# Differential attention in a hybrid encoder: both score maps of a query block in one place, past keys stored in front of new keys

## The reference, cut to what matters

```python
s1 = jnp.einsum('bqhd,bkhd->bhqk', q1, k1).astype(jnp.float32) * scale + bias
s2 = jnp.einsum('bqhd,bkhd->bhqk', q2, k2).astype(jnp.float32) * scale + bias
p = jax.nn.softmax(s1, axis=-1) - lam * jax.nn.softmax(s2, axis=-1)
return jnp.einsum('bhqk,bkhd->bqhd', p.astype(v.dtype), v)
```

## Time and profile before

| | |
|---|---|
| median of three runs | 1973.59 us |
| the profiled execution, its own time | 1973.13 us |
| span in the profile, first to last instruction | 1971.0 us |
| TensorE busy | 1923.3 us, 98% of the span |
| VectorE, ScalarE, GpSimd busy | 65%, 54%, 10% |
| granted TensorE clock, mean | 0.996 |

### The profile page before, as it was taken

The page is one execution under the profiler, slowest core; times in us unless marked ns, Lnnn a source line. Parts: engine busy times, 40 slices in busy tenths (PEclk is TensorE's granted clock), DMA queues, the critical chain, the costliest instruction groups (busy, mean ns, idle before and its releaser), DMA issues.

```text
span 1971.0 us, 37511 instructions
## 1 busy us (share of the span) xinstructions
PE 1923.3 (98%) x15310; PEld 1884.5 (96%) x15310; DVE 1277.1 (65%) x2334; ACT 1061.0 (54%) x1715; POOL 191.2 (10%) x242
## 2 busy tenths in 40 slices
PE   7999999999999999999999999999999999999997
PEld 6999999999998999999989999999999989999997
DVE  6657676765437866666667676767654388666666
ACT  5466666665236644444565757575732475444444
POOL 4312121100110000000041212120001000000000
PEclk9999999999999999999999999999999999999998
DMA  5323232322232332233313232323222323333231
GB/s 139 102 65 111 65 102 71 85 65 86 86 100 72 91 103 87 86 97 94 99 55 100 66 101 73 103 71 85 74 87 86 95 69 95 89 115 87 86 95 60
DMA packets 275710, 172.34 MB, mean 87 GB/s; under 512 B 7592, under 2 KB 271104, under 8 KB 275552
## 3 DMA queue, kind: packets, MB, share of 16 engines
q1 hardware_dynamic: 268000, 155.47, 27.0%
q0 software_dynamic: 7520, 14.59, 2.7%
q10 hardware_dynamic: 32, 0.04, 0.0%
HBM read 158.86 MB, written 11.21 MB: 86 GB/s over the span
## 4 chain that ended last, share of the span: by engine, by line
PE 80%; ACT 9%; DVE 7%; issue 3%; DMA 1%; SPq 0%; ACTq 0%; DVEq 0%
PE PJ L774 34%; PE PJ L1054 19%; PE PX L1115 13%; PE PJ L786 3%; PE PJ L956 3%; PE PX L989 2%; ACT w_hi L1287 2%; DVE w_lo L1842 1%; DVE T L1952 1%; PE PX L1007 1%; PE PX L1027 1%; PE PX L786 1%; DVE uc L2090 1%; DMA w_raw<-in_w_in 1%; ACT L1513 1%
## 5 line engine op out<-in xcount | busy, mean ns | idle before, releaser
L1842 DVE TENSOR_TENSOR w_lo<-w_raw,w_hi 128x1024 fp32r<-128x1024 f32 x236 | 299.2, 1270 | 188.9 <-ACT w_hi L1287 187.9
L1287 ACT ACTIVATE w_hi<-w_raw 128x1024 fp32r<-128x1024 f32 x236 | 247.4, 1052 | 209.9 <-DMA w_raw<-in_w_down 124.5
L774 PE MATMUL PJ<-h_hi,w_hi 128*128 128x272 f32 x1536 | 329.4, 296 | 2.5 <-DVE T L1952 1.9
L774 PE MATMUL PJ<-h_hi,w_lo 128*128 128x272 f32 x1536 | 316.6, 288 | 0.0
L774 PE MATMUL PJ<-h_lo,w_hi 128*128 128x272 f32 x1536 | 315.9, 287 | 0.0
L774 PEld LDWEIGHTS PJ<-h_hi,w_hi 128*128 128x128 f32 x1536 | 239.8, 188 | 10.2 <-issue 7.4
L774 PEld LDWEIGHTS PJ<-h_lo,w_hi 128*128 128x128 f32 x1536 | 240.1, 188 | 0.0
L774 PEld LDWEIGHTS PJ<-h_hi,w_lo 128*128 128x128 f32 x1536 | 239.7, 188 | 0.0
L1054 PE MATMUL PJ<-u_hi,w_hi 128*128 128x272 f32 (+2 forms) x1016 | 215.7, 288 | 0.0
L1054 PE MATMUL PJ<-u_hi,w_lo 128*128 128x272 f32 (+2 forms) x1016 | 214.2, 288 | 0.0
L1054 PE MATMUL PJ<-u_lo,w_hi 128*128 128x272 f32 (+2 forms) x1016 | 213.9, 287 | 0.0
(11 more groups left out here) (413 smaller groups left out, 4771.7 us busy)
## 6 DMA issues: line engine op xcount, KB each, us to landing
w_raw<-in_w_in SPq DMA_DIRECT2D x110, 512.0 KB, 3.8
w_raw<-in_w_down SPq DMA_DIRECT2D x64, 512.0 KB, 3.7
w_raw<-in_w_up SPq DMA_DIRECT2D x62, 512.0 KB, 5.3
w_raw<-in_w_branch_attn SPq DMA_DIRECT2D x16, 512.0 KB, 3.6
w_raw<-in_w_branch_lru SPq DMA_DIRECT2D x16, 512.0 KB, 3.6
w_raw<-in_w_out SPq DMA_DIRECT2D x16, 512.0 KB, 3.6
out_prompt_k<-stage POOLq DMA_DIRECT2D x16, 256.0 KB, 2.8
out_prompt_v<-GA POOLq DMA_DIRECT2D x8, 512.0 KB, 4.5
```

The costliest lines, as they stand in the source:

```text
L774: mm = pe.matmul(PJ[:, buf, half, 0:HT], w[a], src[b][:, k0 + k, HT * half:HT * half + HT], start=first and k == 0 and a + b == 0, stop=en ...
L1287: act.activation(w_hi[:, n.hi, :, :], raw(n), ACT.Copy).then_inc(w_hi_ready, 1)
L1842: dve.tensor_tensor(low(n)[:], raw(n), w_hi[:, n.hi, :, :].bitcast(F32), ALU.subtract).then_inc(w_lo_ready, 1)
```

## The change

Queries and keys get tiles of their own: `q_hi`, `q_lo` hold both maps' queries, and `k_hi`, `k_lo` hold for each map the 256 past keys and behind them the 544 new ones, so that the sample's 288 keys (past and own) are one run of columns. The sample's scores become one set of six matmuls of 288 columns for each map in place of six of 256 and six of 32.

The tables now put S2 and S3 behind half tile 2, and S8 and S9 behind half tile 8. T0, T1 and T4 and the V product W1 stand one half tile later (T0 at 4, T1 at 5, T4 and W1 at 9). S3 and S9 go to PSUM banks 2 and 3, where S1 already went. S9 waits for the low part of T3 and for the placing of W0's result, T0 for the reading of S3, T4 and W1 for the reading of S9. The other conditions stand as they were.

Outside the loop, `sub_ssq` of the first head moves behind the first half of tile 3, next to `turn_k` of the first map, and `turn_k` of the second map moves behind the third value group, next to `sub_ssq` of the second head (in groups p = 0, next to `turn_past`).

```diff
-SCORES_AT = {0: (0, 1), 2: (2,), 3: (3,), 4: (4, 5), 6: (6, 7), 8: (8,), 9: (9,)}
+SCORES_AT = {0: (0, 1), 2: (2, 3), 4: (4, 5), 6: (6, 7), 8: (8, 9)}
...
-            if s == 1:
+            if s in (1, 3, 9):
                 return PX[:, 2 + u, :]
...
+                elif s == 9:
+                    pe.wait_ge(pt_lo_ready, NU * g + 4)
+                    pe.wait_ge(o_placed, NW * g + 1)
                 elif s not in (5, 7):
                     need(pe, biased, 2 * sg, first=p + s == 0)
...
                 if qs == 0:
                     for a, b in ((0, 0), (0, 1), (1, 0)):
                         for u in range(2):
-                            pe.matmul(PX[:, u, 0:PAST], QK[a][R[u], m, 0:P], PK[b][R[u], m, :], start=a + b == 0, stop=a == 1)
-                    for a, b in ((0, 0), (0, 1), (1, 0)):
-                        for u in range(2):
-                            mm = pe.matmul(PX[:, u, PAST:NKS], QK[a][R[u], m, 0:P], QK[b][R[u], 2 + m, 0:NS], start=a + b == 0, stop=a == 1)
+                            mm = pe.matmul(score_at(s, u)[:, 0:NKS], Q[a][R[u], m, 0:P], K[b][R[u], m, 0:NKS], start=a + b == 0, stop=a == 1)
...
-                if t == 0 and p > 0:
-                    pe.wait_ge(o_rs, 4 * g - 1)
+                if t in (0, 4):
+                    pe.wait_ge(biased, 20 * g + (8 if t == 0 else 20))
...
+                if v == 1:
+                    pe.wait_ge(biased, 20 * g + 20)
...
                         gemm(n2, H, 0, 0, n.value + 1)
+                        gemm(n3, H, 0, 1, n.value + 2, ks=range(0, 4))
                         sub_ssq(l, p - 1, 0)
-                        gemm(n3, H, 0, 1, n.value + 2, ks=range(0, 4))
                         turn_k(l, p, 0)
...
-                    v_groups(l, p, (2,))
+                    v_groups(l, p, (2, 3))
                     turn_k(l, p, 1)
-                    v_groups(l, p, (3,))
```

More of the change, by code:

```diff
@@ L60 @@
 UNITS = ((0, (0,)), (0, (1,)), (1, (0,)), (1, (1,)), (2, (0, 1)), (3, (0, 1)), (4, (0, 1)))
-SCORES_AT = {0: (0, 1), 2: (2,), 3: (3,), 4: (4, 5), 6: (6, 7), 8: (8,), 9: (9,)}
-TURN_AT = {3: 0, 4: 1, 6: 2, 7: 3, 8: 4, 10: 5, 11: 6}
-WEIGH_AT = {7: 0, 8: 1, 11: 2, 12: 3}
+SCORES_AT = {0: (0, 1), 2: (2, 3), 4: (4, 5), 6: (6, 7), 8: (8, 9)}
+TURN_AT = {4: 0, 5: 1, 6: 2, 7: 3, 9: 4, 10: 5, 11: 6}
+WEIGH_AT = {7: 0, 9: 1, 11: 2, 12: 3}
 TURNED_BY = (3, 4, 6, 7)
@@ L171, in hybrid_encoder @@
         m_lo = at("m_lo", [P, KT, NT], F32R, BIG + 2 * KT * TILE)
-        qk_hi = at("qk_hi", [P, 4, NT], F32R, BIG + 3 * KT * TILE)
-        qk_lo = at("qk_lo", [P, 4, NT], F32R, BIG + 3 * KT * TILE + 4 * TILE)
+        k_hi = at("k_hi", [P, 2, PAST + NT], F32R, BIG + 3 * KT * TILE)
+        k_lo = at("k_lo", [P, 2, PAST + NT], F32R, BIG + 3 * KT * TILE + 8 * (PAST + NT))
+        q_hi = at("q_hi", [P, 2, NT], F32R, BIG + 3 * KT * TILE + 16 * (PAST + NT))
         GB = at("GB", [P, KT, NT], F32, BIG + 3 * KT * TILE)
@@ L187, in hybrid_encoder @@
         v_hi = at("v_hi", [P, 5, 2, VD], F32R, V_AT)
-        v_lo = at("v_lo", [P, 5, 2, VD], F32R, V_AT + 5120)
-        pk_hi = at("pk_hi", [P, 2, PAST], F32R, V_AT + 10240)
-        pk_lo = at("pk_lo", [P, 2, PAST], F32R, V_AT + 12288)
+        v_lo = at("v_lo", [P, 4, 2, VD], F32R, V_AT + 5120)
+        q_lo = at("q_lo", [P, 2, NT], F32R, V_AT + 9216)
         pv_hi = at("pv_hi", [P, 2, 2 * VD], F32R, V_AT + 14336)
@@ L413, in turned_block, with qk_part @@
             return slice(w * (n * i + kt), w * (n * i + kt) + w)
+        def qk_part(i, lo):
+            return (q_lo if lo else q_hi)[:, i, :] if i < 2 else (k_lo if lo else k_hi)[:, i - 2, PAST:PAST + NT]
         def wide_pt(p, u, lo):
@@ L719, in _ @@
                         pool.wait_ge(qk_hi_ready, 4 * g + i + 1)
-                        pool.tensor_tensor(qk_lo[:, i, :], T[:, i % 2, :], qk_hi[:, i, :].bitcast(F32), ALU.subtract).then_inc(qk_lo_ready, 1)
+                        pool.tensor_tensor(qk_part(i, 1), T[:, i % 2, :], qk_part(i, 0).bitcast(F32), ALU.subtract).then_inc(qk_lo_ready, 1)
                         if i >= 2:
@@ L972, in scores @@
                     need(pe, o_placed, NW * g, first=g == 0)
+                elif s == 9:
+                    pe.wait_ge(pt_lo_ready, NU * g + 4)
+                    pe.wait_ge(o_placed, NW * g + 1)
                 elif s not in (5, 7):
                     need(pe, biased, 2 * sg, first=p + s == 0)
-                QK = (qk_hi, qk_lo)
-                PK = (pk_hi, pk_lo)
+                Q, K = (q_hi, q_lo), (k_hi, k_lo)
                 R = (slice(0, HD), slice(HD, 2 * HD))
@@ L988, in scores @@
                         for u in range(2):
-                            mm = pe.matmul(score_at(s, u)[:, 0:kw], QK[a][R[u], m, cols(qs)], QK[b][R[u], 2 + m, NS:NS + kw], start=a + b == 0, stop=a == 1)
+                            mm = pe.matmul(score_at(s, u)[:, 0:kw], Q[a][R[u], m, cols(qs)], K[b][R[u], m, NKS:NKS + kw], start=a + b == 0, stop=a == 1)
                 mm.then_inc(scores_done, 1)
@@ L1026, in weigh_v @@
                         for a, b in passes:
-                            mm = pe.matmul(PX[:, 3, c], V[a][:, 1 + kt, v, :], wide_pt(p, v, b)[:, kt, c], start=kt + a + b == 0, stop=kt == 3 and a == 1)
+                            mm = pe.matmul(PX[:, 3, c], V[a][:, 1 - a + kt, v, :], wide_pt(p, v, b)[:, kt, c], start=kt + a + b == 0, stop=kt == 3 and a == 1)
                 elif v == 2:
@@ L1031, in weigh_v @@
                             for a, b in passes:
-                                mm = pe.matmul(PX[:, 3, 2 * P * u + P * kt:2 * P * u + 2 * P], V[a][:, 1 + kt, u, :],
+                                mm = pe.matmul(PX[:, 3, 2 * P * u + P * kt:2 * P * u + 2 * P], V[a][:, 1 - a + kt, u, :],
                                                narrow_pt(b)[:, u, (0, 2 * P)[kt]:(2 * P, 3 * P)[kt]], start=kt + a + b == 0, stop=kt == 1 and a == 1)
@@ L1408, in qk_split @@
                 act.wait_ge(evacuated, TL * l + 12 * p + i + 1)
-                act.activation(qk_hi[:, i, :], T[:, i % 2, :], ACT.Copy).then_inc(qk_hi_ready, 1)
+                act.activation(qk_part(i, 0), T[:, i % 2, :], ACT.Copy).then_inc(qk_hi_ready, 1)
             def stage_k(l, p, m):
@@ L1430, in past_split @@
                 act.wait_ge(past_turned, g + 1)
-                act.activation(pk_hi[:], PX[:, 2, :].rearrange("p (m c) -> p m c", m=2), ACT.Copy).then_inc(pk_hi_ready, 1)
+                act.activation(k_hi[:, :, 0:PAST], PX[:, 2, :].rearrange("p (m c) -> p m c", m=2), ACT.Copy).then_inc(pk_hi_ready, 1)
                 act.activation(pv_hi[:], pv_raw[:], ACT.Copy).then_inc(pv_hi_ready, 1)
@@ L1989, in v_split_lo @@
                 dve.wait_ge(v_hi_ready, 2 * g + 1)
-                dve.tensor_tensor(v_lo[:, 1:5, :, :].rearrange("p g u c -> p g (u c)"), v_rows_at(p),
+                dve.tensor_tensor(v_lo[:].rearrange("p g u c -> p g (u c)"), v_rows_at(p),
                                   v_hi[:, 1:5, :, :].rearrange("p g u c -> p g (u c)").bitcast(F32), ALU.subtract).then_inc(v_lo_ready, 1)
@@ L2081, in past_lo @@
                 dve.wait_ge(pk_hi_ready, 4 * l + p + 1)
-                dve.tensor_tensor(pk_lo[:], PX[:, 2, :].rearrange("p (m c) -> p m c", m=2), pk_hi[:].bitcast(F32), ALU.subtract).then_inc(pk_lo_ready, 1)
+                dve.tensor_tensor(k_lo[:, :, 0:PAST], PX[:, 2, :].rearrange("p (m c) -> p m c", m=2), k_hi[:, :, 0:PAST].bitcast(F32), ALU.subtract).then_inc(pk_lo_ready, 1)
             def conv(l, p, u):
```

## The result

The changed kernel took 1992.23 us (median of four runs, 1991.43 to 1993.99) against 1973.55 (four runs, 1972.32 to 1974.04): ratio 1.0098, 95% interval 1.0085 to 1.0111, so 18.7 us slower. The forecast was 1989.7 us, in a range of 1977 to 1996. The profiled execution took 1992.58 us with a span of 1990.2, 19.2 more than before.

What follows compares the result with a forecast made beforehand. TensorE, busy for 98%, was taken to bound the kernel. Eight groups times (2.65 - 0.20) gave +19.6 us, less 3.0 around the loop: +16.6 on 1973.13, so 1989.7 us, with 1977 to 1996 for 8 in 10.

Steps and rivals of the forecast that it cites:

- S3: Scores on TensorE: would wait for VectorE's reading of the scores just ahead, starting 2.51 us after them; some 1.5 us gap.
- the second rival: Paired scores: S3 does not wait, starting 0.64 to 0.70 us after the scores ahead; 1975 us, no change; 4%.
- T1: Second turn on TensorE: would wait 1.04 to 1.24 us, taken as 1.15, for VectorE's low part of the first turn.
- S2 to T2: First part of a group on TensorE: would take 19.3 us in place of 16.68, costing 2.65 us more.
- W1: V product on TensorE: would wait 0.37 to 0.54 us, taken as 0.45, for VectorE's reading of S9.
- T2 to T5: Later part of a group on TensorE: would take 17.6 us, a change of -0.2 us a group.
- the saving of 0.59 at S8 and S9: Sample's scores on TensorE: twelve matmuls of 288 columns in 1.0 us replace 0.79 and 0.80, so -0.59 us a group.
- Around the loop: Moved key turn and sums: 2.4 us saved by the vanished wait, 0.6 by fewer changes of kind; 3.0 in all.
- The sum: Whole kernel: eight groups' +19.6 us less 3.0 around the loop, +16.6, giving 1989.7 us; own range 1985 to 1994.
- Only S3 felt: Attention groups: delays at T1 and W1 are absorbed by a quicker VectorE chain; 12.8 us missing, 1976.9 us; 6%.
- Changes of kind: Borders between 64-row and 128-row matmuls: dearer than counted, deciding from some 1.1 us per removed pair; 1971 at 1.2; 3%.
- The clock in the new holes: S3's hole: TensorE's clock falls once in each group, 3.35 us each, 27 us on top, 2016 us; 5%.

Runs made afterwards that it cites:

- e1: Changed kernel with S3's wait lowered by two reads, so it no longer asks for the reading of the scores just ahead: 1978.13 us, ratio 1.0029 against the kernel before.
- e7: Kernel before with only S3 moved right behind the preceding scores, still writing banks 0 and 1: 1984.99 us, ratio 1.0062.
- e2: Changed kernel with VectorE's low part of the first turn put ahead of the combination of block 1: 1983.66 us, ratio 1.0054 against the kernel before.
- e6: Kernel before with only the moved key turns and sums of squares: 1971.79 us against 1972.32, ratio 0.9995.
- e3: Changed kernel with the reading of S9 put ahead of the combination of block 3, its exponents in their own room: 1986.69 us, ratio 1.0068 against the kernel before.
- e4: Changed kernel with the edits of e1, e2 and e3 together: 1963.36 us, ratio 0.9962 against the kernel before.
- e10: Kernel before with the edits of e5 and e6 together, its three tables unchanged: 1968.08 us against 1972.74, ratio 0.9976.
- e5: Kernel before with only past keys in front of new keys, so S8 and S9 are six matmuls of 288 columns each: 1972.77 us against 1972.32, ratio 0.9998.

## Why the prediction was right

**S3.** Forecast 2.51 us behind S2, measured 2.47; the release took 0.06 us where 0.1 was allowed. e1 and e7 show that the wait alone makes it: put in, it appears with the same 1.51 us; taken out, 1.81 us a group return. Without the wait S3 follows 0.80 us behind S2 and not 0.64 to 0.70 as the second rival has it.

**T1.** Forecast 5.25 to 5.45 us behind S4, measured 5.31 (185.87 to 191.18). S4's reading started 1.54 behind S4 (1.39 to 1.59 forecast); from there to the end of the low part were 3.63 us, not 3.76, and the release took 0.14, not 0.1, so two small errors partly cancelled. T1 came 1.10 us later than an unbroken half tile would have brought it (1.15 taken). e2 shows the order on VectorE to be the cause. S2 to T2 came out at 19.25 us against 19.33.

**W1 was mis-sized.** Forecast: start 4.46 to 4.63 us behind S8, wait 0.45. Measured: 4.73 and 0.64 (the 0.47 in the list of waits is less, since it starts only when the last matmul ahead has drained). S8's reading came in time, 0.91 behind S8. What was missing is in VectorE's rows at 206.67 and 207.71: from S8's reading to S9's were 2.84 us where I had summed 2.59. The 2.59 ends at the low part of T4, which before followed the combination without a pause. S9's reading starts 0.17 us behind the combination's recorded end (207.54), because it waits for `p_ready` of that combination: it overwrites rows of `s2` that the combination reads. W1 also did not get shorter (208.69 to T4 at 210.12 is 1.43 us, as before). So T2 to T5 is 17.81 us (195.55 to 213.36), not 17.6: the saving of 0.59 at S8 and S9 came (0.79 + 0.80 became 1.00) and the wait used it up: T2 to T5 was 17.81 us before as well. Eight times 0.21 is 1.7 us of what the forecast missed.

**Around the loop.** Forecast -3.0 us, measured -2.8, the same when done alone (e6); its two terms, 2.4 for the wait and 0.6 for changes of kind, were not measured apart. The term that an emptied pipeline costs some 0.16 us beyond the gap is borne out at the three new waits: 1.67 us lost for a gap of 1.51 at S3 (2.47 less the 0.80 of e1), 1.10 for 0.94 at T1, 0.64 for 0.47 at W1. ScalarE's key copy was not felt.

**The sum.** Inside the groups +20.6 (19.6 forecast, which over eight groups had S2 to T2 0.6 us too long and T2 to T5 1.7 too short), between -2.8 (-3.0), outside +1.4 (0). The last is within what one execution differs from another, so how near the total came is in part chance; the three waits and the key turn are not.

**The rivals.** Only S3 felt, or S3 not waiting: out by the list of waits. Changes of kind: their price is some 0.4 us for a site that joins another, below the 1.1 from which that rival decides, but not nothing. The clock in the new holes: inside the groups it stayed at full speed, and this is the row of the changed kernel over S3's hole. (The half-speed row is the time behind a fall; in the 3.40 us ahead of it, from 980.50, TensorE had been busy for 1.14.)

```profile
176.30:179.70 3.40, 1.89 (x14) 1.01 (x13) 2.58 (x11) 0.75 (x3) 0.00 (x0) 1.00 0.19 53
```

## What to carry to other kernels

When work is moved to another buffer, go through the counts that it waits for: a semaphore counts events and does not know banks, and a count that was right for the old buffer makes the new one wait for a reader it has no business with. Work that is put together on one engine must be asked for on the other: here VectorE still had a long combination between the two readings that TensorE now wanted back to back, and reordering VectorE (e2, e3) took back 0.43% and 0.28%. With the lower count of e1 as well (e4), a change that lost 0.98% gains 0.38%. Where whole executions differ by 5 us in stretches that the edit does not touch, cut the span at landmarks and compare the pieces.

## What the runs showed of the hardware beside this

TensorE's clock falls in some executions at places where it does not fall in others of the same kernel. The Trainium skill, page "TensorE: Matmul & The Clock Gate", section "What's actually happening", says that the chip's watch over TensorE's activity runs free and does not start anew with a kernel; the three profiles of one program fit that, with an extra half-clock stretch at 609.9 us in one and none there in two. In the stretches above it fell in e10 after TensorE had been busy for 1.48 of 3.40 us, and did not fall after 1.47 of 3.40 in the kernel before.

A site of score matmuls has a fixed part: six of 288 columns took 0.60 us alone (e5), twelve 1.00 (the changed kernel). By these two, if each six cost the same, the fixed part is about 0.20 us, an estimate.
